# An encoder step on one core: the up projections by five matrix products a block in place of six, and the low-rank chunk by its high parts alone

## The chip, the cores and the metric

One core of a Trainium2 chip. The metric is the device time of one execution in microseconds, the median of three runs.

## The reference

Two layers over 544 tokens (512 of a prompt, 32 of a sample), width 1024, float32. Each layer normalises, mixes, adds, normalises again and goes through a gated feed-forward part. The odd layer's mixer has a forget gate of rank 16. Cut to what matters:

```python
def conv_ffn(h, conv_prev, w_up, conv_w, conv_b, w_down):
    gate, val = jnp.split(h @ w_up, 2, axis=-1)
    ext = jnp.concatenate([conv_prev.astype(h.dtype), gate], axis=1)
    conv = conv_b
    for j in range(CONV_W):
        conv = conv + ext[:, j:j + l] * conv_w[j]
    y = (jax.nn.gelu(conv) * val) @ w_down
    return y, ext[:, -(CONV_W - 1):]

# in odd_mixer: cr is h @ w_in's columns 1536 to 1551
log_a = jax.nn.log_sigmoid((cr @ w_gate2 + b_gate).astype(f32)) / GATE_NORM
```

w_up is 1024 x 5632 and w_down 2816 x 1024 in either layer.

## The kernel before

Activations lie with features on the 128 partitions and the 544 tokens along the free axis: a tensor of width 1024 is eight feature blocks of 128 x 544. Weights come as 187 slabs of 128 x 1024, each of which holds eight blocks of 128 x 128. SyncE loads a slab, GpSimd splits it into a high part `w_hi` and a low part `w_lo` (`split`, lines 392 to 395, into a ring of four slabs; it waits until TensorE has done the slab four places earlier), and TensorE multiplies it. All matrix products that use slabs are made of three products in the float32r type: high by high, high weight by low activation, low weight by high activation.

There are two ways to write the three products of one 128 x 128 block:

- `tiles` (lines 424 to 426): the 544 tokens are cut in two halves of 272, each half in a PSUM bank of its own, with three matmuls each, so six a block. All projections but the down projections use it.
- `tiles_apart` (lines 435 to 439): the tokens are cut in 304 (`ONE`) and 240 (`TWO`). The 304 take three matmuls. For the 240, one matmul of 480 columns multiplies the high weight by the high and the low activations side by side, into two separate areas of one bank, and one of 240 adds the low weight's part to the first area. So it is five a block, and whoever reads the result must add the two areas. The down projections use it (lines 1290 to 1294 add both areas to `x`).

An up projection of a layer is 22 gate slabs and 22 value slabs in turn. The four PSUM pairs are used in the order gate, value, gate, value of two chunks; TensorE may overwrite a pair once VectorE has read the chunk two before (`gate_out`, `val_out`). For each chunk VectorE (`ffn`, `chunk`, lines 1236 to 1271) scales the gate by `rstd` into a buffer with two columns of history before the prompt and before the sample, writes those edges, and forms the causal convolution of three taps (L1254, L1256, L1259). ScalarE takes the GELU (L893), VectorE scales the value (L1264), multiplies (L1267, L1268), ScalarE rounds to the high part (L898) and VectorE subtracts for the low part (L1271). Every order is written out by hand; each engine runs its own program and they meet in semaphores.

The odd mixer begins with slab 86, the low-rank chunk `cr`: 16 of its 128 output columns are not zero. Its block c waits until VectorE has written the low part of normalised block c (`norm_low`, L1190, announced by `h_ready`). Then the sum of squares is reduced (`total`, L448), the next slab follows, and behind it the product of the 16 rows of `cr` with the gate's second weight (L654). After slab n = 2 of this mixer VectorE runs, for both halves j of the gate, a prefix sum (L1508) with its subtractions (L1506, L1513), and only then evacuates slab n = 3 (L1480), which slab n = 5 waits for.

Of the kernel before, what the change touches and what calls it, by code (L numbers as in the profile page):

```python
# [22 lines left out]
F32 = mybir.dt.float32  # L23
# [64 lines left out]
def build(nc, io):  # L88
    ctx = ExitStack()
    with ctx:  # L90
# [128 lines left out]
        resets = sq[:, 0]  # L219
        o_s_in = sb("sample_state", [P, 256])  # L220
# [27 lines left out]
        w_hi_done, w_ready = sem("w_hi_done"), sem("w_ready")  # L248
# [26 lines left out]
        og_read, head_y = sem("og_read"), sem("head_y")  # L275
        conv_ready, y_f, y_ready = sem("conv_ready"), sem("y_f"), sem("y_ready")
# [104 lines left out]
        def _(pool):  # L381
# [33 lines left out]
        def _(pe):  # L415
# [59 lines left out]
            def ffn(layer, n_norm, upd0):  # L475
                s0, d0, f0 = S_UP[layer], S_DOWN[layer], FC * layer

                def up(i, k, fresh=False):
# [5 lines left out]
                    tiles(k, s0 + k, h_tiles(0, KC), True, True).then_inc(slab_done, 1)  # L484
# [362 lines left out]
        def _(ac):  # L847
# [37 lines left out]
            def ffn(layer, n_norm, upd0):  # L885
                s0, d0, f0, g0 = S_UP[layer], S_DOWN[layer], FC * layer, sums(n_norm + 1)

                def chunk(i, p):

                    f = 2 * i + p  # L890
                    ac.wait_ge(conv_ready, 2 * i + (f0 + p + 1))
# [121 lines left out]
            dma(o_wg[0:16, :], io["gate_w"], in_odd)  # L1013
# [156 lines left out]
        def _(ve):  # L1170
# [59 lines left out]
            def ffn(layer, n_norm, upd0):  # L1230
                s0, d0, f0 = S_UP[layer], S_DOWN[layer], FC * layer

                def chunk(i, p):
# [11 lines left out]
                    grouped(g, 2 * p, 2).then_inc(gate_out, 1)  # L1245
# [3 lines left out]
                    ve.tensor_copy(g[:, SEQ + 2:SEQ + 4].unsqueeze(1), conv_past[:, layer, one, :]).then_inc(vec, 1)  # L1249
# [555 lines left out]
```

## Time and profile before

| | us |
|---|---|
| median of 3 runs | 1280.73 |
| lowest and highest of them | 1280.19, 1281.85 |
| the profiled execution | 1279.63 |
| its span in the trace | 1277.5 |
| TensorE busy | 1223.4 (96% of the span) |
| VectorE busy | 807.4 (63%) |
| GpSimd busy | 699.6 (55%) |
| ScalarE busy | 261.8 (20%) |

A row of the timeline gives the start and the length of an instruction; matmuls overlap in it, so the pace of TensorE is the distance between starts, or a stretch divided by its count of matmuls. In a row of groups the mean of one instruction stands behind the busy time, and behind the bar stands the idle time of that engine before the group. L with a number is a line of the kernel before.

### The profile page before, as it was taken

How to read it: one execution, taken by the hardware profiler on the slowest of the kernel's cores; microseconds unless marked ns; L12 is line 12 of the kernel's file. 1: busy time of each engine (PE TensorE's matmuls, PEld its weight loads, DVE VectorE, ACT ScalarE, POOL GpSimd, SP SyncE). 2: the span in 40 equal slices, each digit the busy share in tenths (PEclk: the TensorE clock that was granted, in tenths of full speed). 3: DMA queues.
4: the chain of work that ended last, by engine and by line, in shares of the span. 5: the costliest groups of instructions: out<-in, count | busy, mean ns of one | idle time of the engine just before them, and what ended most of it. 6: DMA issues, size and time to landing. Idle time of an engine off the chain costs nothing.

```text
span 1277.5 us, 24157 instructions
## 1 busy us (share of the span) xinstructions
PE 1223.4 (96%) x9325; PEld 1178.8 (92%) x9325; DVE 807.4 (63%) x1206; ACT 261.8 (20%) x514; POOL 699.6 (55%) x565
## 2 busy tenths in 40 slices
PE   6978899999999999999999998899999999999995
PEld 6967799999999999999999986799999999999995
DVE  6987577778787731126534688766777777762222
ACT  3015332111111200002111165422111111110002
POOL 6732257655665666665653441256665566566661
PEclk9989999999999999999999999999999999999998
DMA  5311123222222223223222310132222222222221
GB/s 212 116 58 34 32 71 100 82 82 96 85 82 86 94 83 100 99 94 115 84 83 67 102 50 33 34 110 85 97 82 82 89 92 82 83 98 93 90 81 71
DMA packets 35522, 108.88 MB, mean 85 GB/s; under 512 B 5984, under 2 KB 7792, under 8 KB 35472
## 3 DMA queue, kind: packets, MB, share of 16 engines
q1 hardware_dynamic: 29232, 102.51, 24.0%
q10 hardware_dynamic: 6240, 5.64, 1.4%
q8 instruction: 39, 0.64, 0.2%
q14 instruction: 11, 0.09, 0.0%
HBM read 103.00 MB, written 5.13 MB: 85 GB/s over the span
## 4 chain that ended last, share of the span: by engine, by line
PE 87%; DVE 9%; ACT 2%; issue 1%; DMA 0%; POOL 0%; ACTq 0%; POOLq 0%; SPq 0%; DVEq 0%
PE psum L424 21%; PE psum L426 20%; PE psum L425 20%; PE psum L437 6%; PE psum L435 4%; PE psum L436 4%; PE psum L438 4%; PE psum L439 3%; DVE even_winsum L1358 1%; PE psum L754 1%; PE psum L621 1%; DVE small L1579 1%; DVE even_rope_swapped L1340 1%; ACT diff_probs L1091 0%; DVE even_diff L1361 0%
## 5 line engine op out<-in xcount | busy, mean ns | idle before, releaser
L424 PE MATMUL psum<-h_hi,w_hi 128*128 128x272 f32 x2032 | 593.7, 292 | 14.4 <-DVE h_lo L1190 10.3
L426 PE MATMUL psum<-h_hi,w_lo 128*128 128x272 f32 x2032 | 588.8, 290 | 0.0
L425 PE MATMUL psum<-h_lo,w_hi 128*128 128x272 f32 x2032 | 585.8, 288 | 0.0
L395 POOL TENSOR_TENSOR w_lo<-w_raw,w_hi 128x1024 fp32r<-128x1024 f32 x187 | 465.1, 2487 | 15.6
L424 PEld LDWEIGHTS psum<-h_hi,w_hi 128*128 128x128 f32 x2032 | 383.2, 189 | 19.6 <-issue 16.7
L425 PEld LDWEIGHTS psum<-h_lo,w_hi 128*128 128x128 f32 x2032 | 383.9, 189 | 0.2
L426 PEld LDWEIGHTS psum<-h_hi,w_lo 128*128 128x128 f32 x2032 | 383.1, 189 | 0.0
L392 POOL TENSOR_TENSOR tick<-tick 1x1 f32<-1x1 f32 x183 | 38.5, 210 | 523.7 <-PE psum L426 444.4
L393 POOL TENSOR_SCALAR w_hi<-w_raw 128x1024 fp32r<-128x1024 f32 x187 | 197.5, 1056 | 9.3 <-DMA w_raw<-in_weights 8.0
L437 PE MATMUL psum<-y_both,w_hi 128*128 128x480 f32 x352 | 133.4, 379 | 0.0
L1290 DVE TENSOR_TENSOR x<-x,psum 128x240 f32 (+1 forms) x16 | 6.4, 401 | 176.1 <-PE psum L439 176.0
L1254 DVE TENSOR_SCALAR conv<-gate,consts 128x546 f32<-128x546 f32 x44 | 104.1, 2366 | 7.0 <-DVE tails L1251 6.9
L435 PE MATMUL psum<-y_both,w_hi 128*128 128x304 f32 x352 | 107.7, 306 | 0.0
L436 PE MATMUL psum<-y_both,w_hi 128*128 128x304 f32 x352 | 106.4, 302 | 0.0
L438 PE MATMUL psum<-y_both,w_lo 128*128 128x304 f32 x352 | 105.4, 300 | 0.0
L439 PE MATMUL psum<-y_both,w_lo 128*128 128x240 f32 x352 | 95.7, 272 | 0.0
L1267 DVE TENSOR_TENSOR sq<-sq,conv 128x512 f32<-128x512 f32 x44 | 65.3, 1483 | 43.7 <-ACT conv L893 43.7
L439 PEld LDWEIGHTS psum<-y_both,w_lo 128*128 128x128 f32 x352 | 66.0, 188 | 10.2
L436 PEld LDWEIGHTS psum<-y_both,w_hi 128*128 128x128 f32 x352 | 66.9, 190 | 0.0
L437 PEld LDWEIGHTS psum<-y_both,w_hi 128*128 128x128 f32 x352 | 66.2, 188 | 0.0
L438 PEld LDWEIGHTS psum<-y_both,w_lo 128*128 128x128 f32 x352 | 66.1, 188 | 0.0
L435 PEld LDWEIGHTS psum<-y_both,w_hi 128*128 128x128 f32 x352 | 66.1, 188 | 0.0
(217 smaller groups left out, 1456.1 us busy)
## 6 DMA issues: line engine op xcount, KB each, us to landing
w_raw<-in_weights SPq DMA_DIRECT2D x187, 512.0 KB, 3.5
x<-in_x SPq DMA_DIRECT2D x8, 272.0 KB, 5.6
out_y<-x SPq DMA_DIRECT2D x8, 272.0 KB, 2.4
out_diff_v_new<-odd_dv ACTq DMA_DIRECT2D x1, 1024.0 KB, 6.2
out_diff_k_new<-odd_kT ACTq DMA_DIRECT2D x1, 1024.0 KB, 4.7
even_rope<-in_rope ACTq DMA_DIRECT2D x1, 544.0 KB, 3.9
odd_rope<-in_rope ACTq DMA_DIRECT2D x1, 544.0 KB, 3.6
consts<-in_consts ACTq DMA_DIRECT2D x1, 384.5 KB, 4.7
```

The costliest lines, as they stand in the source:

```text
L393: pool.tensor_scalar(w_hi[:, k], w_raw[:, k % RAW], 1.0, 0.0, ALU.mult, ALU.add).then_inc(w_hi_done, 1)
L395: pool.tensor_tensor(w_lo[:, k], w_raw[:, k % RAW], w_hi[:, k].bitcast(F32), ALU.subtract).then_inc(w_ready, 1)
L424: pe.matmul(out, wh, xh[:, cols], start=first and n == 0, stop=False)
L425: pe.matmul(out, wh, xl[:, cols], start=False, stop=False)
L426: ins = pe.matmul(out, wl, xh[:, cols], start=False, stop=last and n == len(pairs) - 1)
L435: pe.matmul(one, wh, both[:, 0, 0:ONE], start=first, stop=False)
L436: pe.matmul(one, wh, both[:, 1, 0:ONE], start=False, stop=False)
L437: pe.matmul(two, wh, both[:, :, ONE:T], start=first, stop=False)
L438: pe.matmul(one, wl, both[:, 0, 0:ONE], start=False, stop=last)
L439: return pe.matmul(two[:, 0], wl, both[:, 0, ONE:T], start=False, stop=last)
L1254: ve.tensor_scalar(c[:, :], g[:, 0:CO], tap(0), None, ALU.mult).then_inc(vec, 1)
L1267: ve.tensor_tensor(sq[:, p, 0:SEQ], sq[:, p, 0:SEQ], c[:, 0:SEQ], ALU.mult)
```

## The change

Four edits:

1. All slabs of the up projections go through `tiles_apart` (h's high and low parts become one tensor `h_both`). The value and the gate thus have a second area of 240 columns. ScalarE copies it from PSUM to SBUF (`gate_rest`, `val_rest`, in the space of `sumsq`), VectorE adds the copy to the first area in PSUM (`fold`) and scales from there.
2. The first tap moves from VectorE (L1254) to ScalarE, which waits for the edge columns (`edge_in`) and is waited for by the second tap (`tap_ready`).
3. The low-rank chunk: its weights are written twice, in columns 0 to 15 and 32 to 47. GpSimd overwrites the second copy's high part with the low part (one instruction, `stacked`), so four matmuls a block with 48 weight columns stand in for six. Rows 0 to 15 and 32 to 47 of the result are added in the gate's product, whose weight is stacked twice too.
4. The prefix sum of the gate's second half runs after slab n = 3 is evacuated, not before.

```diff
@@ gpsimd
-            with pool.Fori(1, NSLAB // RING) as i:
+            first_odd = S_ODD_IN // RING
+            with pool.Fori(1, first_odd + 1) as i:
+                for k in range(RING):
+                    split(i, k)
+            pool.wait_ge(w_ready, S_ODD_IN + 1)
+            cr = S_ODD_IN % RING
+            pool.tensor_scalar(w_hi[:, cr].rearrange("p (c m) -> p c m", c=KC)[:, :, 32:48],
+                               w_lo[:, cr].bitcast(F32).rearrange("p (c m) -> p c m", c=KC)[:, :, 0:16],
+                               1.0, 0.0, ALU.mult, ALU.add).then_inc(stacked, 1)
+            with pool.Fori(first_odd + 1, NSLAB // RING) as i:
@@ tensor
+            def low_rank(acc, s, c):
+                wh = w_hi[:, s % RING, c * P:c * P + 48]
+                for half in range(2):
+                    cols = slice(half * HALF, (half + 1) * HALF)
+                    out = psum[0:48, 2 * acc + half, 0:HALF]
+                    pe.matmul(out, wh, h_hi[:, c, cols], start=c == 0, stop=False)
+                    ins = pe.matmul(out, wh, h_lo[:, c, cols], start=False, stop=c == KC - 1)
+                return ins
...
+                    if n_norm and n == 0:
+                        pe.wait_ge(stacked, 1)
...
-                    tiles(k, s0 + k, h_tiles(0, KC), True, True).then_inc(slab_done, 1)
+                    for c in range(KC):
+                        ins = tiles_apart(k, s0 + k, c, h_both[:, :, c], c == 0, c == KC - 1)
+                    ins.then_inc(slab_done, 1)
...
-                        ins = tiles(k, s0 + k, h_tiles(c, c + 1), c == 0, c == KC - 1)
+                        ins = tiles_apart(k, s0 + k, c, h_both[:, :, c], c == 0, c == KC - 1)
@@ scalar, chunk of ffn
+                    ac.wait_ge(slab_done, 4 * i + (s0 + 2 * p + 1))
+                    ac.activation(gate_rest, psum[:, 4 * p + 1, TWO:2 * TWO], ACT.Copy).then_inc(gate_apart, 1)
+                    ac.wait_ge(edge_in, 2 * i + (f0 + p + 1))
+                    ac.activation(conv[p][:, :], gate[p][:, 0:CO], ACT.Copy,
+                                  scale=conv_w[:, layer, one, 0]).then_inc(tap_ready, 1)
...
+                    ac.wait_ge(slab_done, 4 * i + (s0 + 2 * p + 2))
+                    ac.activation(val_rest, psum[:, 4 * p + 3, TWO:2 * TWO], ACT.Copy).then_inc(val_apart, 1)
@@ vector, chunk of ffn
+                def fold(acc, rest):
+                    two = psum[:, 2 * acc + 1, 0:TWO]
+                    ve.tensor_tensor(two, two, rest, ALU.add).then_inc(vec, 1)
+                    return two
...
-                    grouped(g, 2 * p, 2).then_inc(gate_out, 1)
+                    ve.tensor_tensor(g[:, 2:2 + ONE], psum[:, 4 * p, 0:ONE], rstd[:, 0:ONE], ALU.mult)
+                    ve.wait_ge(gate_apart, 2 * i + (f0 + p + 1))
+                    two = fold(2 * p, gate_rest)
+                    ve.wait_ge(vec, at_ + 1)
+                    ve.tensor_tensor(g[:, 2 + ONE:2 + SEQ], two[:, 0:SEQ - ONE], rstd[:, ONE:SEQ], ALU.mult)
+                    ve.tensor_tensor(g[:, SEQ + 4:GE], two[:, SEQ - ONE:TWO], rstd[:, SEQ:T], ALU.mult).then_inc(gate_out, 1)
...
-                    ve.tensor_scalar(c[:, :], g[:, 0:CO], tap(0), None, ALU.mult).then_inc(vec, 1)
-                    ve.wait_ge(vec, at_ + 4)
+                    ve.wait_ge(tap_ready, 2 * i + (f0 + p + 1))
...
-                    ve.tensor_tensor(halves(sq[:, p]), pair(2 * p + 1), halves(rstd), ALU.mult).then_inc(val_out, 1)
+                    ve.tensor_tensor(sq[:, p, 0:ONE], psum[:, 4 * p + 2, 0:ONE], rstd[:, 0:ONE], ALU.mult)
+                    ve.wait_ge(val_apart, 2 * i + (f0 + p + 1))
+                    two = fold(2 * p + 1, val_rest)
+                    ve.wait_ge(vec, at_ + 5)
+                    ve.tensor_tensor(sq[:, p, ONE:T], two, rstd[:, ONE:T], ALU.mult).then_inc(val_out, 1)
@@ vector, odd mixer
-                if n == 2:
-                    for j in range(2):
+                if n in (2, 3):
+                    for j in (n - 2,):
```

The order of ScalarE in its loop over chunks, first of the two chunks of an iteration; `conv_61` and `conv_60` are the same convolution buffer. Before:

```order
L893 ISA [waits in_const,conv_ready]
L893 ACT_TABLE_LOAD
L893 ACTIVATE conv_61<-conv_61,consts 128x546
L898 ISA [waits in_const,y_f]
L898 ACTIVATE y_both<-sq 128x544
```

Now:

```order
L923 ACT_TABLE_LOAD
L923 ACTIVATE sumsq<-psum 128x240 [waits slab_done]
L924 ISA
L926 ISA [waits in_const,edge_in]
L926 ACTIVATE conv_60<-gate_58,consts 128x546
L930 ISA [waits in_const,conv_ready]
L930 ACT_TABLE_LOAD
L930 ACTIVATE conv_60<-conv_60,consts 128x546
L933 REGISTER_ALU
L934 ACTIVATE sumsq<-psum 128x240 [waits slab_done]
L937 ISA [waits in_const,y_f]
L937 ACTIVATE y_both<-sq 128x544
```

The copies and the first tap have come in, and a second table load stands ahead of the first copy; the copy of the value's area stands behind the GELU. The second chunk of an iteration has no table load, before and now.

The order of VectorE in the odd mixer about slabs n = 2 and n = 3; `gate_tmp_101` and `gate_tmp_102` before, `gate_tmp_100` and `gate_tmp_101` now, are the two halves of the gate. Before:

```order
L1478 SCALAR_TENSOR_TENSOR odd_gla_q<-psum,rstd 128x544 [waits slab_done]
L1506 SCALAR_TENSOR_TENSOR gate_tmp_101<-gate_tmp_101 128x544 [waits gate_l]
L1508 SCALAR_TENSOR_TENSOR gate_tmp_101<-sq,gate_tmp_101 128x544 [waits vec]
L1513 TENSOR_TENSOR gate_tmp_101<-gate_tmp_101 128x512 [waits vec]
L1513 TENSOR_TENSOR gate_tmp_101<-gate_tmp_101 128x32
L1506 SCALAR_TENSOR_TENSOR gate_tmp_102<-gate_tmp_102 128x544 [waits gate_l]
L1508 SCALAR_TENSOR_TENSOR gate_tmp_102<-sq,gate_tmp_102 128x544 [waits vec]
L1513 TENSOR_TENSOR gate_tmp_102<-gate_tmp_102 128x512 [waits vec]
L1513 TENSOR_TENSOR gate_tmp_102<-gate_tmp_102 128x32
L1480 TENSOR_TENSOR odd_gla_k<-psum,rstd 128x544 [waits slab_done] x2
```

Now:

```order
L1531 SCALAR_TENSOR_TENSOR odd_gla_q<-psum,rstd 128x544 [waits slab_done]
L1559 SCALAR_TENSOR_TENSOR gate_tmp_100<-gate_tmp_100 128x544 [waits gate_l]
L1561 SCALAR_TENSOR_TENSOR gate_tmp_100<-sq,gate_tmp_100 128x544 [waits vec]
L1566 TENSOR_TENSOR gate_tmp_100<-gate_tmp_100 128x512 [waits vec]
L1566 TENSOR_TENSOR gate_tmp_100<-gate_tmp_100 128x32
L1533 TENSOR_TENSOR odd_gla_k<-psum,rstd 128x544 [waits slab_done]
L1559 SCALAR_TENSOR_TENSOR gate_tmp_101<-gate_tmp_101 128x544 [waits gate_l]
L1561 SCALAR_TENSOR_TENSOR gate_tmp_101<-sq,gate_tmp_101 128x544 [waits vec]
L1566 TENSOR_TENSOR gate_tmp_101<-gate_tmp_101 128x512 [waits vec]
L1566 TENSOR_TENSOR gate_tmp_101<-gate_tmp_101 128x32
L1533 TENSOR_TENSOR odd_gla_k<-psum,rstd 128x544 [waits slab_done]
```

The evacuation of slab n = 3 now stands between the work on the two halves; that of n = 4 stands behind both, as before.

## Rows read from the trace of the kernel before

**Rows 1.** The page: its first line, and the chain that ended last, by engine.
```profile
span 1277.5 us, 24157 instructions
...
PE 87%; DVE 9%; ACT 2%; issue 1%; DMA 0%; POOL 0%; ACTq 0%; POOLq 0%; SPq 0%; DVEq 0%
```

**Rows 2.** TensorE in four stretches: up and down of either layer (length, busy, matmuls).
```profile
200.00:440.00 240.00, 240.00 (x1905) 1.00 0.27 87
450.00:570.00 120.00, 120.00 (x805) 1.00 0.29 97
885.00:1125.00 240.00, 240.00 (x1906) 1.00 0.26 87
1135.00:1255.00 120.00, 120.00 (x806) 1.00 0.26 83
```

**Rows 3.** Groups of VectorE while layer 0 projects up, 200 to 440 us.
```profile
L1254 DVE TENSOR_SCALAR conv<-gate,consts 128x546 f32<-128x546 f32 x20 | 47.2, 2358 | 3.2 <-DVE tails L1251 3.2
L1267 DVE TENSOR_TENSOR sq<-sq,conv 128x512 f32<-128x512 f32 x20 | 28.7, 1436 | 19.9 <-ACT conv L893 19.9
L1268 DVE TENSOR_TENSOR sq<-sq,conv 128x32 f32<-128x32 f32 x20 | 25.5, 1277 | 0.0
...
L1249 DVE COPY gate<-consts 128x2 f32 x19 | 10.0, 528 | 3.0 <-DVE gate L1200 3.0
```

**Rows 4.** Single lines of VectorE, all 44 times: shortest/median/longest ns.
```profile
L1254 DVE TENSOR_SCALAR conv<-gate,consts x44: 505/2452/2584, 195.2 to 1132.2; 128x546 f32<-128x546 f32 x44
...
L1267 DVE TENSOR_TENSOR sq<-sq,conv x44: 692/1056/2186, 202.5 to 1137.5; 128x512 f32<-128x512 f32 x44
...
L1268 DVE TENSOR_TENSOR sq<-sq,conv x44: 176/1279/2386, 203.1 to 1138.4; 128x32 f32<-128x32 f32 x44
```

**Rows 5.** Groups of ScalarE in the same stretch.
```profile
L893 ACT ACTIVATE conv<-conv,consts 128x546 f32<-128x546 f32 x20 | 15.1, 754 | 68.8 <-DVE conv L1259 68.7
L893 ACT ACT_TABLE_LOAD x11 | 14.1, 1283 | 79.6 <-DVE conv L1259 79.6
L898 ACT ACTIVATE y_both<-sq 128x544 f32 x20 | 13.2, 658 | 57.3 <-DVE sq L1268 57.3
```

**Rows 6.** Timeline about 308 us: GpSimd first, then VectorE (start us, us).
```profile
306.83 0.18 POOL L392 TENSOR_TENSOR tick<-tick 1x1 f32<-1x1 f32 x1 [2.39 <-PE psum L426]
...
308.11 2.70 POOL L395 TENSOR_TENSOR w_lo<-w_raw,w_hi 128x1024 fp32r<-128x1024 f32 x1
...
308.49 2.38 DVE L1268 TENSOR_TENSOR sq<-sq,conv 128x32 f32<-128x32 f32 x1
...
312.48 0.85 DVE L1200 TENSOR_TENSOR gate<-psum,rstd 128x272 f32<-128x272 f32 x3
```

**Rows 7.** Timeline of the first chunk of layer 1: VectorE, then TensorE.
```profile
578.14 0.46 DVE L1291 TENSOR_TENSOR x<-x,psum 128x304 f32 x1
578.52 0.39 DVE L1294 TENSOR_TENSOR x<-x,psum 128x240 f32 x1
580.19 1.83 DVE L1190 SCALAR_TENSOR_TENSOR h_lo<-x,consts,h_hi  x1 [1.28 <-ACT h_hi L863]
581.94 0.71 DVE L1181 TENSOR_TENSOR sumsq<-sumsq,sq 128x544 f32<-128x544 f32 x1
...
577.23 0.29 PE L424 MATMUL psum<-h_hi,w_hi 128*128 128x272 f32 x1
...
583.28 1.08 PE L448 MATMUL psum<-sumsq,consts 128*128 128x272 f32 x4
```

**Rows 8.** Timeline of the gate's scans: VectorE, then TensorE.
```profile
600.57 3.37 DVE L1508 TENSOR_TENSOR_SCAN gate_tmp<-sq,gate_tmp 128x544 f32<-128x544 f32 x1
...
610.36 1.34 DVE L1480 TENSOR_TENSOR odd_gla_k<-psum,rstd 128x544 f32<-128x544 f32 x2
...
610.50 0.29 PE L426 MATMUL psum<-h_hi,w_lo 128*128 128x272 f32 x1
611.22 0.36 PE L424 MATMUL psum<-h_hi,w_hi 128*128 128x272 f32 x1 [0.43 <-DVE odd_gla_k L1480]
```

More of the change, by code:

```diff
@@ L106, in build @@
         h_at = top[0]
-        h_hi = sb("h_hi", [P, KC, T], F32R)
-        h_lo_at = top[0]
-        h_lo = sb("h_lo", [P, KC, T], F32R)
+        h_both = sb("h_both", [P, 2, KC, T], F32R)
+        h_lo_at = h_at + KC * T * 4
+        h_hi, h_lo = h_both[:, 0], h_both[:, 1]
         y_at = top[0]
@@ L460, in in_projection @@
                             pe.wait_ge(h_ready, KC * n_norm + c + 1)
-                        ins = tiles(in_acc(n_norm == 0, n), s0 + n, h_tiles(c, c + 1), c == 0, c == KC - 1)
+                        if n_norm and n == 0:
+                            ins = low_rank(in_acc(False, n), s0 + n, c)
+                        else:
+                            ins = tiles(in_acc(n_norm == 0, n), s0 + n, h_tiles(c, c + 1), c == 0, c == KC - 1)
                         if n_norm == 0 and n == 2 and c == 1:
@@ L653, in odd_side @@
                         for half in range(2):
-                            ins = pe.matmul(psum[:, 2 * j + half, 0:HALF], o_wg[0:16, j * P:(j + 1) * P],
-                                            o_cr[0:16, half * HALF:(half + 1) * HALF], start=True, stop=True)
+                            ins = pe.matmul(psum[:, 2 * j + half, 0:HALF], o_wg[0:48, j * P:(j + 1) * P],
+                                            o_cr[0:48, half * HALF:(half + 1) * HALF], start=True, stop=True)
                     ins.then_inc(side_mm, 1)
@@ L890, in chunk @@
                     f = 2 * i + p
+                    one = slice(f, f + 1) if isinstance(i, int) else bass.ds(f, 1)
+                    ac.wait_ge(slab_done, 4 * i + (s0 + 2 * p + 1))
+                    ac.activation(gate_rest, psum[:, 4 * p + 1, TWO:2 * TWO], ACT.Copy).then_inc(gate_apart, 1)
+                    ac.wait_ge(edge_in, 2 * i + (f0 + p + 1))
+                    settle(ac)
+                    ac.activation(conv[p][:, :], gate[p][:, 0:CO], ACT.Copy,
+                                  scale=conv_w[:, layer, one, 0]).then_inc(tap_ready, 1)
                     ac.wait_ge(conv_ready, 2 * i + (f0 + p + 1))
@@ L1244, in chunk @@
                     settle(ve)
[L1245 removed]
+                    at_ = 10 * i + (vec0 + 5 * p)
+                    ve.tensor_tensor(g[:, 2:2 + ONE], psum[:, 4 * p, 0:ONE], rstd[:, 0:ONE], ALU.mult)
[4 more added lines that the diff above has]
+                    ve.tensor_tensor(g[:, SEQ + 4:GE], two[:, SEQ - ONE:TWO], rstd[:, SEQ:T], ALU.mult).then_inc(gate_out, 1)
                     ve.wait_ge(gate_out, 2 * i + (f0 + p + 1))
                     settle(ve)
[L1249 removed]
+                    ve.tensor_copy(g[:, SEQ + 2:SEQ + 4].unsqueeze(1), conv_past[:, layer, one, :]).then_inc(edge_in, 1)
                     ve.tensor_copy(tails[:, one, 0:2], g[:, SEQ:SEQ + 2].unsqueeze(1)).then_inc(vec, 1)
                     ve.tensor_copy(tails[:, one, 2:4], g[:, GE - 2:GE].unsqueeze(1)).then_inc(vec, 1)
[L1252 removed]
                     ve.wait_ge(vec, at_ + 3)
[L1254 to L1255 removed]
+                    ve.wait_ge(tap_ready, 2 * i + (f0 + p + 1))
                     ve.scalar_tensor_tensor(c[:, :], g[:, 1:1 + CO], tap(1), c[:, :], ALU.mult, ALU.add)\
                         .then_inc(vec, 1)
[L1258 removed]
+                    ve.wait_ge(vec, at_ + 4)
                     ve.scalar_tensor_tensor(c[:, :], g[:, 2:2 + CO], tap(2), c[:, :], ALU.mult, ALU.add)\
@@ L1767, in lay_out @@
     out["rope"] = rope.reshape(P, 2, T)
-    out["gate_w"] = f["gla_w_gate2"][0]
+    out["gate_w"] = np.zeros((48, 256), np.float32)
+    out["gate_w"][0:16] = out["gate_w"][32:48] = f["gla_w_gate2"][0]
     out["lambda"] = np.ascontiguousarray(np.broadcast_to(f["diff_lambda"][0].reshape(1, 256), (P, 256)))
```

15 lines of the change are left out of this document (8 added, 7 removed).

## The prediction

> **What bounds the kernel now.** I read the page's chain first: 87% of what ended last is TensorE, 9% VectorE [rows 1]. So an edit pays if it shortens TensorE's stream or one of its few waits, and costs if it makes TensorE wait. Next the stretches by engine: in both projections of the feed-forward part TensorE is busy all the time at a granted clock of 1.00, the 2.4 GHz level, so its pace is the length of a stretch over its matmuls [rows 2]. Then what runs beside it there: VectorE and ScalarE [rows 3 to 6]. Last the two places of the odd mixer that the other edits touch [rows 7, 8].
>
> **Edit 1, TensorE's side.** Going up takes 240 us for 1905 matmuls, 126.0 ns each; six make a block, so 755.9 ns. Going down takes 120 us for 805, 149.1 ns each; five make a block, 745.3 ns. Layer 1 reads the same (1906 and 806) [rows 2]. Both forms stream as many columns: 6 x 272 = 1632 and 3 x 304 + 480 + 240 = 1632. At 2.4 columns per ns that is 680 ns, so what is left is 12.7 ns per matmul in one form and 13.1 in the other: the change saves one such remainder a block, 10.6 ns. The up projections have 2 layers x 44 slabs x 8 blocks = 704 blocks: **7.5 us**, all on the path. It is the same instruction form on the same engine with operands of the same kind, so I take the down row as it is; the bounds are 10.6 and 12.7 ns a block, 7.5 to 8.9 us, if TensorE waits for nobody.
>
> The Trainium skill has a rule against this: "TensorE: Matmul & The Clock Gate", Back-to-back issue gap, gives a single matmul's gap as N/2.4 + 2.5 ns. By it a matmul saved is worth 2.5 ns, an estimate of 1.8 us in all instead of 7.5. The trace's down row disagrees, and the row decides.
>
> **Edits 1 and 2, VectorE's and ScalarE's side.** Does TensorE then wait? A chunk is two slabs, 16 blocks: 12.1 us before, 11.93 after. VectorE's gate read of the eleventh chunk starts at 312.48, while its slab ended just before GpSimd's small instruction at 306.83 [rows 6]: VectorE runs some 6 us behind, and reads without waiting for TensorE. TensorE waits for a buffer only two chunks on, so this has cost nothing.
>
> VectorE's chunk of 12.1 us holds waits that stand in the rows as long durations. L1254 takes 2.36 us on average and 0.51 at least, L1267 1.44 and 0.69, L1268 (32 columns) 1.28 and 0.18, L1249 (two columns) 0.53 against some 0.29 [rows 3, 4]. In the timeline L1268 starts at 308.49 and ends at 310.87, just as GpSimd's L395 ends at 310.81 [rows 6]. So such instructions sit out GpSimd's pass over the weights. They add 1.85 + 0.75 + 1.10 + 0.24 = 3.9 us, which leaves a bare chain of 8.2 us.
>
> What the change does to the bare chain, per chunk:
> - L1254 goes from VectorE: -0.5 bare, and 1.85 of sitting out with it.
> - The gate read was 0.85 in three pieces [rows 6]. It becomes 304 columns, 0.46, the fold of 240, 0.39, then 208 and 32 columns, at most 0.39 and 0.18 [rows 4, 7], with a handover of 0.1: +0.65.
> - The second tap waits for ScalarE's first tap, 0.75 [rows 5] with two handovers, less the two edge copies that run meanwhile: +0.65.
> - Value: VectorE now waits for GELU (0.75, in every second chunk behind a table load of 1.28) and behind it for the copy, about 0.4 (an estimate from 0.66 for 544 columns) [rows 5], and then folds and scales, 0.39 each [rows 7]. Start to product it was 0.72 plus an idle time of 19.9/20 = 1.0 [rows 3]; it becomes 2.9: +1.2.
> - A second table load per two chunks stands ahead of the gate's copy. It begins when ScalarE has rounded, VectorE is then busy for about 1.2 us with L1271 and 304 columns, and 1.28 + 0.4 are needed: +0.5 every second time, +0.25.
>
> The sum is 8.2 - 0.5 + 0.65 + 0.65 + 1.2 + 0.25 = 10.45 us bare, below 11.93 by 1.5. With the remaining waits on GpSimd at today's mean (2.1) it would be 12.5, above it. I take the first as the measure, for this reason: GpSimd's pass over slab s + 4 starts when TensorE has done slab s, so an instruction that sits it out ends at a time fixed by TensorE, however late VectorE was. A late VectorE waits less. I worked one pair of chunks through: the edge copy falls into L395 and ends with it, L1267 falls into the next L395, and each next gate read starts 0.3 to 2.2 us late against its place, without growing. So the lag stays near 6 to 8 us. Now val_out comes about 10.3 us after the gate read starts, and it is needed four slabs (23.9 us) after the gate's slab ends, so the lag may be 13.6. Cost: **0**, with VectorE's lateness hidden by the two spare buffers. The copies of the low parts and ScalarE's other work have room: it works 15.1 + 14.1 + 13.2 = 42 of these 240 us [rows 5].
>
> The down projection needs the last chunk only behind its first two accumulators' 16 blocks each, 24 us later; nothing there. GpSimd has one more small instruction and leaves its loop once; it rests 2.39 us a slab [rows 6] and is three slabs ahead: 0.
>
> **Edit 3.** 48 matmuls become 32: 16 x 126.0 ns = 2.0 us less of TensorE. But each block waits for its h_lo. The first block starts at 577.23 and the last h_lo is there at 580.19 + 1.83 = 582.02; before, block 8 began at 577.23 + 7 x 0.756 = 582.52 and did not wait. At 0.504 a block it would begin at 580.76, so it waits until 582.1 and ends at 582.6. Then L448 needs the sum of squares, ready at 581.94 + 0.71 = 582.65. It starts at 582.8 instead of 583.28 [rows 7]: **0.5 us**. The other 1.5 become a wait for VectorE. Bounds: 0.3 if a handover is slow, 2.0 if both chains before it move too.
>
> **Edit 4.** TensorE's gap before slab n = 5 is 611.22 - 610.50 = 0.72, less the usual 0.13: 0.6 us, ended by L1480 at 610.36, which stood behind both prefix sums [rows 8]. Now that evacuation stands between them. Next late would be the evacuation of n = 4, at 610 to 612.5, needed by TensorE only near 616. **0.6 us**; bounds 0 and 0.7.
>
> **Sum.** 7.5 + 0.5 + 0.6 = 8.6 us. The profiled execution took 1279.63 us around a span of 1277.5 and becomes 1271.0. It lay 1.1 below the median of 1280.73, so the median becomes **1272.1**.
>
> **Rivals.**
> A. VectorE's chain bounds the up stage, slower than before. Place: the second and third tap, which read two SBUF tensors, also fall into GpSimd's first pass (about 1.05 us), and the edge copy and L1267 keep sitting out at their mean. Then a chunk takes 12.5 + 1.0 = 13.5. A layer has 20 chunks after the first two; the lag may grow by 13.6 - 6 = 7.6 us before TensorE stalls: 20 x (13.5 - 11.93) - 7.6 = 24 us a layer, 48 in two, less 8.6: 1320. It decides from 12.3 us a chunk, and from 12.5 it eats the whole gain. For it: rows 3 show such waits on more than one line. Against it: the fixed end of each. 6%.
> The Trainium skill, "SBUF — State Buffer", Who interferes with whom, says that a VectorE instruction with two SBUF inputs contends with a GpSimd one that reads SBUF and blocks fully; the trace agrees for L1267 and L1268. By that rule the taps can be blocked too.
> B. The same with all waits at today's mean, 12.5 us a chunk: 20 x 0.57 - 7.6 = 3.8 us a layer, 7.6 in two, so 1279.7, no change that shows. 4%.
> C. The joined matmul of 480 gives less here than in the down projection, for example a fifth of the remainder of 12.7 ns: 1.8 + 1.1 = 2.9 us, 1277.8. For it nothing in the trace; against it rows 2. The same small figure follows if the edit did not do what it says; the row counts would show it. 4%.
> D. The low-rank chunk gives its full 2.0, and a saved block 12 ns in place of 10.6: 8.4 + 2.0 + 0.6 = 11.0, 1269.7. For it: the waits in rows 7 hang on a VectorE instruction of 1.83 that also sat out GpSimd. Against it: nothing ahead of it moves. 8%.
> The forecast itself has 78%: 1270.7 to 1273.5 with the bounds of edits 3 and 4 and of the runs' own spread.
>
> **How the numbers follow.** I predict 1272.1. The range takes in the forecast, most of D below, and above it small stalls up to half of B: 1269.8 to 1276.0. About 0.2% (2.6 us) is what a measurement of this kernel can tell from no change. The forecast, C and D are faster by more than that: 0.90. Within 0.2% is B: 0.04. Slower is A: 0.06.
>
> **What would show it.** In the trace of the changed kernel: the up stretch with five matmuls in 745 ns and no idle time (a block at 756 means C); the sum's matmul L448 about 5.5 us behind the first block of the low-rank chunk, where it was 6.05, with a wait of about 1.3 us before its last block; no gap before slab n = 5; on VectorE a chunk of 11.93 us, with the lag behind TensorE not growing past 13 us. The prediction is wrong if TensorE shows waits for gate_out or val_out (A, B), or if the first slabs of the up stage wait.

## The result and the profile after

| | before | changed |
|---|---|---|
| median, same comparison (us) | 1280.48 | 1288.28 |
| runs | 6 | 6 |
| profiled execution: span (us) | 1277.5 | 1286.6 |

The ratio is 1.006, 95% interval 1.005 to 1.007: slower by 7.8 us, which is small, under 1%, but clear of the noise. The forecast was 1272.1 us, with a range of 1269.8 to 1276.0.

The page of the changed kernel: its first line, the busy line of the engines, and the shares of the chain.

```profile
span 1286.6 us, 23189 instructions
...
PE 1219.6 (95%) x8605; PEld 1153.0 (90%) x8605; DVE 748.0 (58%) x1294; ACT 348.3 (27%) x668; POOL 718.4 (56%) x566
...
PE 87%; DVE 8%; ACT 2%; issue 2%; DMA 0%; POOL 0%; ACTq 0%; POOLq 0%; DVEq 0%; SPq 0%
```

TensorE's busy time fell by 3.8 us only, from 1223.4, and the span grew by 9.1, from 1277.5. So there is new idle time, and matmuls that ran slowly. TensorE by stretches, columns as in [rows 2] (length, busy, matmuls, granted clock):

```profile
200.00:440.00 240.00, 240.00 (x1610) 1.00 0.27 88
447.50:453.50 6.00, 6.00 (x23) 0.53 0.24 81
460.00:570.00 110.00, 110.00 (x738) 1.00 0.29 96
890.00:1130.00 240.00, 240.00 (x1610) 1.00 0.27 88
```

Up goes at 240/1610 = 149.1 ns a matmul, five a block, 745.3 ns, exactly the down row's pace [rows 2]; layer 1 reads the same. But in the six microseconds from 447.5 the granted clock is 0.53, little above its 1.2 GHz level, and only 23 matmuls fit; in the kernel before, the same six microseconds hold 42. TensorE's timeline where layer 0 turns from up to down:

```profile
441.82 0.27 PE L452 MATMUL psum<-h_both,w_lo 128*128 128x240 f32 x1
447.35 0.59 PE L448 MATMUL psum<-y_both,w_hi 128*128 128x304 f32 x1 [5.25 <-issue]
447.74 0.46 PE L449 MATMUL psum<-y_both,w_hi 128*128 128x304 f32 x1
```

The last matmul of up starts at 441.82, the first of down at 447.35. Five and a half microseconds of waiting, after which matmuls start 0.39 apart instead of 0.14. From the start of the last up block to that of the first of down it is 6.17 us, then from block to block 1.49, 1.38, 1.37, 1.37, 0.83 and 0.75 from there on: the first six take 12.6 us where 4.5 are due, so 8.1 are lost. Layer 1 has the same wait, 5.52 us from 1131.23. Two times 8.1 is 16.3 us. Whom did TensorE wait for? VectorE on chunk 20, the last but one:

```profile
436.63 0.47 DVE L1291 TENSOR_TENSOR gate<-psum,rstd 128x304 f32<-128x304 f32 x1
...
438.60 1.66 DVE L1300 COPY gate<-consts 128x2 f32 x1 [0.17 <-DVE gate L1296]
...
441.40 0.79 DVE L1305 SCALAR_TENSOR_TENSOR conv<-gate,consts,conv 128x546 f32<-128x546 f32 x1 [1.00 <-ACT conv L926]
442.33 1.61 DVE L1308 SCALAR_TENSOR_TENSOR conv<-gate,consts,conv 128x546 f32<-128x546 f32 x1
443.87 0.46 DVE L1313 TENSOR_TENSOR sq<-psum,rstd 128x304 f32<-128x304 f32 x1
446.39 0.42 DVE L1275 TENSOR_TENSOR psum<-psum,sumsq 128x240 f32<-128x240 f32 x1 [2.06 <-ACT sumsq L934]
446.84 0.41 DVE L1317 TENSOR_TENSOR sq<-psum,rstd 128x240 f32<-128x240 f32 x1
```

L1291 begins to read the gate, L1300 is the edge copy, L1305 and L1308 are the two taps, and L1317 scales the value's second part and announces `val_out` at 447.25. TensorE starts 0.1 us later. The same two ends, gate read and value read of chunk 20, in the kernel before:

```profile
433.54 0.84 DVE L1200 TENSOR_TENSOR gate<-psum,rstd 128x272 f32<-128x272 f32 x3
...
439.80 0.72 DVE L1264 TENSOR_TENSOR sq<-psum,rstd 128x544 f32<-128x544 f32 x1
```

There the value was read by 440.5, with TensorE going up until 445.8: a margin of 5.3 us. The line of the kernel that makes this a wait is in `down`, and is in both kernels: both accumulators of down, when j is 0 or 1, wait for `val_out` of chunk 20.

The totals are the matmuls that reduce the sum of squares (L448 before, L471 after; the last one of all is L838 before and L868 after). The distances between their starts divide the time better than the medians do, since the first 190 us alone ranged from 190.1 to 193.2 us over the profiled executions of these kernels. Worked out from the traces, one execution each:

| kernel | up and down of layer 0 | odd mixer | up and down of layer 1 |
|---|---|---|---|
| before | 392.62 | 291.97 | 386.57 |
| changed | 396.84 | 292.57 | 391.38 |
| e1_split | 388.69 | 292.60 | 383.21 |
| e2_late | 402.11 | 293.65 | 394.77 |
| e3_hoist | 394.49 | 292.46 | 390.20 |
| e4_hoist_split | 394.51 | 292.55 | 389.00 |
| f1_tap_back | 395.61 | 292.55 | 390.15 |
| f2_no_folds | 388.69 | 292.92 | 383.21 |
| f3_split_no_odd | 389.27 | 291.60 | 383.21 |
| f4_split_hoist | 388.70 | 292.87 | 383.21 |
| g1_edge_act | 388.68 | 292.84 | 383.21 |
| g2_no_e4 | 388.68 | 291.75 | 383.22 |
| g3_no_e3 | 389.27 | 292.25 | 383.22 |

The first column also holds the odd mixer's low-rank chunk.

### The profile page after: what moved, and what is told of

The parts are those of the page before. It is cut to its first block, busy times and chain, and to the rows that moved or that the text cites. A ratio compares the mean times of both kernels' runs of the same rounds, so it can differ in the third digit from the quotient of the medians.

```text
span 1286.6 us, 23189 instructions
## 1 busy us (share of the span) xinstructions
PE 1219.6 (95%) x8605; PEld 1153.0 (90%) x8605; DVE 748.0 (58%) x1294; ACT 348.3 (27%) x668; POOL 718.4 (56%) x566
## 4 chain that ended last, share of the span: by engine, by line
PE 87%; DVE 8%; ACT 2%; issue 2%; DMA 0%; POOL 0%; ACTq 0%; POOLq 0%; DVEq 0%; SPq 0%
PE psum L450 18%; PE psum L448 12%; PE psum L449 12%; PE psum L451 11%; PE psum L452 9%; PE psum L437 7%; PE psum L439 6%; PE psum L438 6%; DVE even_winsum L1411 1%; PE psum L784 1%; PE psum L651 1%; DVE small L1632 1%; DVE even_rope_swapped L1393 1%; ACT diff_probs L1130 0%; DVE even_diff L1414 0%
## 5 line engine op out<-in xcount | busy, mean ns | idle before, releaser
L398 POOL TENSOR_TENSOR w_lo<-w_raw,w_hi 128x1024 fp32r<-128x1024 f32 x187 | 476.5, 2548 | 15.6
L450 PE MATMUL psum<-h_both,w_hi 128*128 128x480 f32 x704 | 267.0, 379 | 0.0
L448 PE MATMUL psum<-h_both,w_hi 128*128 128x304 f32 x704 | 215.8, 307 | 0.0
L449 PE MATMUL psum<-h_both,w_hi 128*128 128x304 f32 x704 | 212.9, 302 | 0.0
L451 PE MATMUL psum<-h_both,w_lo 128*128 128x304 f32 x704 | 210.9, 300 | 0.0
L437 PE MATMUL psum<-h_both,w_hi 128*128 128x272 f32 x608 | 180.5, 297 | 14.5 <-DVE h_both L1229 10.8
L452 PE MATMUL psum<-h_both,w_lo 128*128 128x240 f32 x704 | 191.5, 272 | 0.0
L439 PE MATMUL psum<-h_both,w_lo 128*128 128x272 f32 x608 | 176.4, 290 | 0.0
L438 PE MATMUL psum<-h_both,w_hi 128*128 128x272 f32 x608 | 175.5, 289 | 0.0
L452 PEld LDWEIGHTS psum<-h_both,w_lo 128*128 128x128 f32 x704 | 131.8, 187 | 20.3
L449 PEld LDWEIGHTS psum<-h_both,w_hi 128*128 128x128 f32 x704 | 133.7, 190 | 0.1
L437 PEld LDWEIGHTS psum<-h_both,w_hi 128*128 128x128 f32 x608 | 115.0, 189 | 19.4 <-issue 16.2
L448 PEld LDWEIGHTS psum<-h_both,w_hi 128*128 128x128 f32 x704 | 132.3, 188 | 0.1
L450 PEld LDWEIGHTS psum<-h_both,w_hi 128*128 128x128 f32 x704 | 132.3, 188 | 0.0
L451 PEld LDWEIGHTS psum<-h_both,w_lo 128*128 128x128 f32 x704 | 132.2, 188 | 0.0
L448 PE MATMUL psum<-y_both,w_hi 128*128 128x304 f32 x352 | 109.4, 311 | 10.5 <-issue 10.5
L438 PEld LDWEIGHTS psum<-h_both,w_hi 128*128 128x128 f32 x608 | 115.3, 190 | 0.1
L439 PEld LDWEIGHTS psum<-h_both,w_lo 128*128 128x128 f32 x608 | 115.0, 189 | 0.0
```

The source lines that it names most:

```text
L398: pool.tensor_tensor(w_lo[:, k], w_raw[:, k % RAW], w_hi[:, k].bitcast(F32), ALU.subtract).then_inc(w_ready, 1)
L437: pe.matmul(out, wh, xh[:, cols], start=first and n == 0, stop=False)
L438: pe.matmul(out, wh, xl[:, cols], start=False, stop=False)
L439: ins = pe.matmul(out, wl, xh[:, cols], start=False, stop=last and n == len(pairs) - 1)
L448: pe.matmul(one, wh, both[:, 0, 0:ONE], start=first, stop=False)
L449: pe.matmul(one, wh, both[:, 1, 0:ONE], start=False, stop=False)
```

## The experiments

The lag, below, is the time from the end of a chunk's gate slab to the start of VectorE's read of it. Theory 1: the whole loss is the wait for the value read of chunk 20, and the slow clock behind it. Rivals: VectorE is too slow for the stage and TensorE will wait for it elsewhere; or ScalarE's tap, not the folds, is what made VectorE late.

**e1_split.** The changed kernel, with the two accumulators' waits told apart. The first overwrites the banks of chunk 20's gate, the second those of its value, 16 blocks later.

```diff
-                                pe.wait_ge(val_out, f0 + FC - 1)
+                                pe.wait_ge(val_out if j else gate_out, f0 + FC - 1)
```

> The changed kernel; the first accumulator of the down projection waits for the gate read of chunk 20 (gate_out), the second for its value read (val_out); before, both waited for the value read. Theory 1 (the whole loss is this wait: VectorE reads that value 5.5 us after the last up matmul, and TensorE then runs five blocks at the lower clock; from 441.8 us on six block distances take 12.6 us where 4.5 are due, 8.1 us a layer): 1288.3 - 16.3 = 1272.0. Rival (VectorE is simply too slow for the stage, and TensorE will wait for it elsewhere, on y_ready or on buffers): 1280 or more.

Measured: 1272.79 us against 1280.36, ratio 0.9939 (0.9923 to 0.9956). TensorE at the same turn, and under it VectorE's gate and value reads of chunk 20:

```profile
442.38 0.27 PE L452 MATMUL psum<-h_both,w_lo 128*128 128x240 f32 x1
442.49 0.30 PE L448 MATMUL psum<-y_both,w_hi 128*128 128x304 f32 x1
442.63 0.30 PE L449 MATMUL psum<-y_both,w_hi 128*128 128x304 f32 x1
```

```profile
437.18 0.47 DVE L1291 TENSOR_TENSOR gate<-psum,rstd 128x304 f32<-128x304 f32 x1
...
447.40 0.41 DVE L1317 TENSOR_TENSOR sq<-psum,rstd 128x240 f32<-128x240 f32 x1
```

Down follows up at the usual 0.11 us. VectorE is as late as in the changed kernel, its value read ends at 447.81, 5.3 us after down began, and nobody waits for it: the second accumulator begins at 442.49 + 16 x 0.746 = 454.4. The up-and-down stretches are shorter than the changed kernel's by 8.15 and 8.17 us, as worked out above. Theory 1 holds, and this version is faster than both kernels.

**e2_late.** The kernel before, with a wait at this place and nothing else of the change.

```diff
-                                pe.wait_ge(val_out, f0 + FC - 1)
+                                pe.wait_ge(val_out, f0 + FC)
```

> The kernel before, whose down projection waits for the value read of chunk 21 in place of chunk 20. Prices an idle time of TensorE at this place without any of the change's edits. VectorE reads that value at 452.5, TensorE arrives at 445.7: 6.9 us of waiting. Theory 1 (a wait here costs its length and then some 2.6 us at the lower clock): 2 x 9.5 = 19 us, 1299.5. Rival (the slow blocks in the changed kernel have another cause, for example late y_ready): 2 x 6.9 = 14 us, 1294.3.

Measured: 1300.39 us against 1280.36, ratio 1.0159 (1.0142 to 1.0176).

```profile
446.74 0.29 PE L426 MATMUL psum<-h_hi,w_lo 128*128 128x272 f32 x1
453.63 0.59 PE L435 MATMUL psum<-y_both,w_hi 128*128 128x304 f32 x1 [6.60 <-issue]
```

A wait of 6.9 us cost 402.11 - 392.62 = 9.5 us in layer 0, so 2.6 went to slow blocks, as expected. In layer 1, with the same 6.9, it was 8.2. In the six microseconds from the first matmul of down the granted clock was 0.52 in layer 0 and 0.76 in layer 1. So the slow blocks belong to the wait, not to the new kernel. Over all the traces with a wait here, what came on top of it varied from 1.3 to 2.7 us.

**e3_hoist.** The changed kernel with ScalarE's GELU table loaded ahead of the loop. Copy is in that table too, so none is left inside.

```diff
                 rms(n_norm, 3)
+                load_tables(11)
                 with ac.Fori(0, FC // 2) as i:
```

> The changed kernel with one table load ahead of ScalarE's loop over chunks and none inside (both functions are in that table). In even chunks the value read then ends 1.3 us earlier and the gate read 0.4. Theory 1a (VectorE's place is held by GpSimd's passes, 12 to 13 us behind its slab): the stall falls from 5.5 to some 4 us a layer, 1285 to 1286. Theory 1b (the two loads in the first chunk are what made VectorE fall a whole pass further behind): the lag is 6 us again, no stall, 1272.

Measured: 1284.75 us against 1280.36, ratio 1.0038 (1.0024 to 1.0052).

```profile
441.83 0.27 PE L452 MATMUL psum<-h_both,w_lo 128*128 128x240 f32 x1
446.09 0.52 PE L448 MATMUL psum<-y_both,w_hi 128*128 128x304 f32 x1 [3.99 <-issue]
```

The wait falls by 1.27 us, one table load, and no more. VectorE's lag (reckoned from the start of up at 5.965 us a slab) is 12.9 to 13.3 us; in the changed kernel it went to and fro between 12.9 and 14.4. So the loads explain the last microsecond of it, and not the pass by which VectorE is late.

**e4_hoist_split** is, against its name, the same kernel as e3_hoist a second time.

> The same kernel as e3_hoist once more, for one look at how alike two traces of one kernel are in VectorE's lag. Both theories: the same lag as in e3_hoist within 0.5 us, time within 0.3%.

Measured, in one run: 1285.3 us, the wait 4.30 against 4.26, the lags equal within 0.2 us. So the lag is no accident of one execution. What the wait costs is less steady: layer 1 took 389.00 us here and 390.20 in e3_hoist, with the same wait of 4.26.

**f1_tap_back.** The changed kernel with edit 2 undone.

```diff
-                    ac.wait_ge(edge_in, 2 * i + (f0 + p + 1))
-                    settle(ac)
-                    ac.activation(conv[p][:, :], gate[p][:, 0:CO], ACT.Copy,
-                                  scale=conv_w[:, layer, one, 0]).then_inc(tap_ready, 1)
...
+                    ve.tensor_scalar(c[:, :], g[:, 0:CO], tap(0), None, ALU.mult).then_inc(tap_ready, 1)
```

> The changed kernel with the first tap back on VectorE, and ScalarE without it (edit 2 undone). Theory 1 (VectorE's added wait for GELU, copy and fold at the value, 3.6 us, and a first chunk that ends one GpSimd pass later, put the value read behind the end of the up stage): the tap's place matters little, since the 2.8 us from edge copy to second tap become an edge copy and a tap that sit out GpSimd; stall 4 to 7 us a layer, 1285 to 1291. Rival (the handover to ScalarE for the tap is what costs the pass): the lag is 6 us, no stall, 1272.

Measured: 1287.0 us against 1280.55, ratio 1.0049 (1.0033 to 1.0064).

```profile
442.65 0.27 PE L452 MATMUL psum<-h_both,w_lo 128*128 128x240 f32 x1
448.18 0.59 PE L448 MATMUL psum<-y_both,w_hi 128*128 128x304 f32 x1 [5.26 <-issue]
```

In layer 0 it is 5.53 us again, and the lag 13 to 14. In layer 1 the lag settles at 12.9 to 13.3 and the wait is 4.46 us (1130.81 to 1135.27). So with the first tap on VectorE a stall of 4.5 to 5.5 us stays: the handover to ScalarE is not what makes it.

**f2_no_folds.** ScalarE's two copies and VectorE's two folds are left out, so a part of the low products of 240 tokens is missing from the result.

```diff
-                    ve.wait_ge(gate_apart, 2 * i + (f0 + p + 1))
-                    two = fold(2 * p, gate_rest)
-                    ve.wait_ge(vec, at_ + 1)
+                    two = psum[:, 4 * p + 1, 0:TWO]
```

> The changed kernel without ScalarE's copies and VectorE's folds; the second area of 240 columns is not added, so its low parts are left out of the result. The tap stays on ScalarE. Theory 1: the value read ends some 3 us earlier after its gate read and ScalarE has one table load per two chunks again; no stall at the start of down, 1271 to 1273. Rival (the tap's handover): the stall stays at 3 us or more a layer, 1281 or more.

Measured: 1274.56 us against 1280.55, ratio 0.9947 (0.9932 to 0.9962), 1.6 us above the expected 1273 at most, a miss of the time; the profiled execution's first total starts at 193.15, where e1_split's starts at 190.69, and its up-and-down stretches equal e1_split's. No wait at down. VectorE's first two gate reads:

```profile
195.76 0.48 DVE L1287 TENSOR_TENSOR gate<-psum,rstd 128x304 f32<-128x304 f32 x1 [6.94 <-ACT rstd L904]
...
206.71 0.47 DVE L1287 TENSOR_TENSOR gate<-psum,rstd 128x304 f32<-128x304 f32 x1
```

Here the first chunk takes 10.95 us, in the changed kernel 16.3. From the third chunk on the lag is 6.0 to 6.7, a whole slab less, with the tap still on ScalarE. So the copies and folds, with what they bring along, are enough to make VectorE late, and the tap alone is not. They are not the only thing that can be taken away: g1_edge_act below keeps them and has the short lag.

**f4_split_hoist.** e1_split with e3_hoist's edit.

> The kernel e1_split with one table load ahead of ScalarE's loop and none inside. Theory 1: once TensorE waits for nobody at the start of down, VectorE's lag costs nothing, so the loads are free: 1272.8, the same as e1_split within 0.5 us. Rival (the lag still costs TensorE somewhere): 1 us or more faster.

Measured: 1273.77 us, ratio 0.9948 (0.9935 to 0.9962), 1.0 us above e1_split where 0.5 at most was expected. The interval overlaps e1_split's, and the profiled execution's first total starts 1.0 us later (191.71 against 190.69). The up-and-down stretches equal e1_split's within 0.01 us. The loads are free once nobody waits, and so is the lag.

**g1_edge_act.** e3_hoist, with the edge copy on ScalarE.

```diff
+                    settle(ac)
+                    ac.activation(gate[p][:, SEQ + 2:SEQ + 4].unsqueeze(1), conv_past[:, layer, one, :],
+                                  ACT.Copy).then_inc(edge_in, 1)
                     ac.wait_ge(edge_in, 2 * i + (f0 + p + 1))
+                    ac.wait_ge(gate_out, 2 * i + (f0 + p + 1))
...
-                    ve.tensor_copy(g[:, SEQ + 2:SEQ + 4].unsqueeze(1), conv_past[:, layer, one, :]).then_inc(edge_in, 1)
```

> The kernel e3_hoist (down still waits for the value read) with the copy of the two edge columns of the gate moved from VectorE to ScalarE, ahead of its first tap; the tap then waits for gate_out. Theory P (VectorE's place two slabs behind is held by the edge copy, which sits out GpSimd's pass for 1.5 us each time): VectorE catches up, its lag falls to 7 us or less, no stall, 1272 to 1273. Rival (another instruction that reads two SBUF tensors, the second or third tap, takes the place of the copy at the same pass): the lag stays at 11 to 13 us and the stall at 2.5 to 4.3 us a layer, 1281 to 1285.

Measured: 1273.86 us against 1281.76, ratio 0.9948 (0.9933 to 0.9962). VectorE at the first chunk, then at chunk 20:

```profile
194.09 0.48 DVE L1296 TENSOR_TENSOR gate<-psum,rstd 128x304 f32<-128x304 f32 x1 [6.94 <-ACT rstd L904]
...
196.67 1.62 DVE L1305 COPY tails<-gate 128x2 f32<-128x2 f32 x1
...
199.22 1.60 DVE L1312 SCALAR_TENSOR_TENSOR conv<-gate,consts,conv 128x546 f32<-128x546 f32 x1
...
205.19 0.47 DVE L1296 TENSOR_TENSOR gate<-psum,rstd 128x304 f32<-128x304 f32 x1
```

```profile
431.54 0.47 DVE L1296 TENSOR_TENSOR gate<-psum,rstd 128x304 f32<-128x304 f32 x1
...
438.94 0.41 DVE L1321 TENSOR_TENSOR sq<-psum,rstd 128x240 f32<-128x240 f32 x1
```

No stall, lag 6.4 to 6.7. Theory P forecast the time, but its mechanism is only half right. The next copy (L1305, two columns of `tails`) takes the edge copy's place and sits GpSimd out just as long, 1.62 us and later 2.3. What changed is that the second tap no longer waits for a ScalarE tap that waits for that copy: it starts 4.3 us behind the first gate read, where it was 5.2 in e3_hoist. The first chunk then ends after 11.1 us instead of 16.0, a pass of GpSimd earlier, and VectorE stays one pass further ahead from there on.

Where that pass is won or lost can be seen on the third tap of the first chunk (L1308 in the changed kernel, L1312 here) and on GpSimd's L398, the pass that reads the weights for the low part. In the changed kernel and here:

```profile
198.55 2.75 POOL L398 TENSOR_TENSOR w_lo<-w_raw,w_hi 128x1024 fp32r<-128x1024 f32 x1
```

```profile
200.32 2.75 POOL L398 TENSOR_TENSOR w_lo<-w_raw,w_hi 128x1024 fp32r<-128x1024 f32 x1
```

In the changed kernel the third tap starts at 199.08, 0.53 us behind the start of L398, and takes 2.81 us. Here it starts at 199.22, 1.1 us ahead of L398, and takes 1.60. All 26 first chunks in the traces (13 kernels, two layers) fall the same way. In the 18 where the tap comes 0.5 us behind the start of L398 it takes 2.81 and the lag is the long one; in the 8 where it comes 1.0 to 1.1 us ahead (the kernel before, e2_late, f2_no_folds and this one) it takes 1.45 to 1.60 and the lag is the short one. f1_tap_back, which has no tap on ScalarE, is among the 18: its second tap took 1.59 us, where g1_edge_act's took 0.79. So the lag is set in the first chunk and then kept. That the third tap's start decides it is read from the traces; no run moved that tap alone.

**f3_split_no_odd, g2_no_e4, g3_no_e3.** These are e1_split with both edits 3 and 4 undone (f3), with only edit 4 undone (g2) and with only edit 3 undone (g3). Below, the first cut undoes edit 4; the second is the main line of what undoes edit 3.

```diff
-                if n in (2, 3):
-                    for j in (n - 2,):
+                if n == 2:
+                    for j in range(2):
...
-                        if n_norm and n == 0:
-                            ins = low_rank(in_acc(False, n), s0 + n, c)
-                        else:
-                            ins = tiles(in_acc(n_norm == 0, n), s0 + n, h_tiles(c, c + 1), c == 0, c == KC - 1)
+                        ins = tiles(in_acc(n_norm == 0, n), s0 + n, h_tiles(c, c + 1), c == 0, c == KC - 1)
```

> The kernel e1_split with edits 3 and 4 undone (low-rank chunk by six matmuls of 128 weight columns a block; both prefix sums behind slab n = 2). The prediction's terms: edit 3 is worth 0.5 us, edit 4 0.6, so 1.1 us above e1_split: 1273.9. In the trace the distance from the odd mixer's first matmul to its second slab is 6.76 again, and the gap before slab n = 5 0.72. Rival (edit 3 gives the full 2.0): 2.6 us above, 1275.4.

> The kernel e1_split with edit 4 alone undone. From total to total, the odd mixer with its attention takes 291.97 us in the kernel before, 292.57 in the changed kernel, 292.60 in e1_split and 291.60 in f3_split_no_odd, though TensorE is 0.6 us ahead at slab n = 5 in the second and third. Theory (edit 4 gives 0.66 there, and the attention, which meets GpSimd's passes 0.6 us earlier, gives back 1.4): this stretch takes 291.6 to 292.0 again and the time is 1271.6 to 1272.5. Rival (edit 3's shift does it): 293.2, and 1273.4.

> The kernel e1_split with edit 3 alone undone. Theory of g2: the stretch from total to total still takes 292.6, and the first chunk of the odd mixer costs 0.6 us more: 1273.4. Rival: the stretch takes 291.0, 1271.7.

Measured: 1273.55 (ratio 0.9944, 0.9931 to 0.9958), 1274.14 (0.9949, 0.9936 to 0.9962) and 1274.08 (0.9944, 0.9931 to 0.9956). The intervals of all three and of e1_split overlap, so by the medians neither edit is worth anything that shows; g2_no_e4 missed its expected 1271.6 to 1272.5, and g3_no_e3 came 0.7 above its 1273.4. The stretches say more. Edit 3 is worth 389.27 - 388.69 = 0.58 us, in two pairs alike. With edit 4 TensorE runs 0.6 us ahead after slab n = 5, and yet the odd mixer takes 292.60 with it (e1_split) and 291.75 without (g2_no_e4). e1_split keeps its lead until 236 us behind the start of this stretch, in the attention, and then loses 1.5 us. Below are a window of e1_split and one of g2_no_e4 at the same work: length; busy time and count of TensorE's matmuls, its weight loads, VectorE, ScalarE and GpSimd; then the granted clock and the DMA:

```profile
816.10:819.50 3.40, 3.40 (x15) 2.66 (x16) 1.51 (x5) 1.13 (x8) 0.00 (x0) 0.50 0.34 140
816.30:819.70 3.40, 3.40 (x22) 2.43 (x22) 2.19 (x8) 1.87 (x10) 0.00 (x0) 1.00 0.54 154
```

The granted clock was 0.50, the 1.2 GHz level, in e1_split and 1.00 in g2_no_e4: 15 matmuls against 22, and GpSimd does nothing in either window. So what was expected, an attention that meets GpSimd's passes at a worse moment, is not what the trace shows there. Such stretches at 0.50 stand in the odd mixer of every trace but f3_split_no_odd's, which has the shortest mixer (291.60); e2_late, with 293.65, and f2_no_folds, with 292.92, have the most. Whether edit 4 brings them on stays open: e2_late's odd mixer is the kernel before's own code, and it took 293.65 where the kernel before took 291.97. The mixer's length moves by that much with what came before it.

## Why the prediction was wrong

**TensorE's gain from edit 1** was right in kind and pace: 745.3 ns a block, the down row's. In the stretches it is 386.57 - 383.21 = 3.36 us in layer 1 where 3.73 were reckoned, so 6.7 us in both instead of 7.5. Rival C is refuted by the 745.3 ns. So is the estimate of 1.8 us from the Trainium skill, "TensorE: Matmul & The Clock Gate", Back-to-back issue gap; the section gives the formula behind it for an isolated matmul, and a matmul saved in this stream was worth about 10 ns.

**The step that failed** is "The down projection needs the last chunk only behind its first two accumulators' 16 blocks each, 24 us later; nothing there." It looked at `y_ready` alone. The line beside it makes the first block of down wait for the value read of chunk 20. Inside up, a pair is needed again four slabs after the gate's slab ends, 23.9 us; at the end of up, the first down block comes after three, 17.9 us. The bound on VectorE's lag was therefore not 13.6 us but 17.9 - 10.3 = 7.6. The runs show what it cost: a wait of 5.5 us at the first block of down in either layer, and 8.15 us a layer in all, which e1_split takes away by that one line. The prediction's own sign of being wrong, a wait for `val_out`, did come, but at down and not inside up.

**The second miss is the size of the lag.** The prediction put it near 6 to 8 us. It was 12.9 to 14.4. The value read came 10.6 us after the gate read of chunk 20 (436.63 to 447.25), as reckoned (10.3), and the groups of VectorE over the same stretch as [rows 3] are near the sum too:

```profile
L1308 DVE SCALAR_TENSOR_TENSOR conv<-gate,consts,conv 128x546 f32<-128x546 f32 x20 | 32.6, 1628 | 2.7 <-DVE conv L1305 0.2
L1300 DVE COPY gate<-consts 128x2 f32 x19 | 26.5, 1394 | 3.1 <-DVE gate L1296 3.1
L1275 DVE TENSOR_TENSOR psum<-psum,sumsq 128x240 f32<-128x240 f32 x40 | 16.5, 412 | 32.9 <-ACT sumsq L934 28.6 <-ACT sumsq L923 4.3
...
L1320 DVE TENSOR_TENSOR sq<-sq,conv 128x512 f32<-128x512 f32 x20 | 15.9, 797 | 0.7
```

L1308, the last tap, and L1300, the edge copy, now sit out GpSimd (1.63 and 1.39 us on average where 0.79 and 0.17 are their shortest), and little else does: some 2.2 us a chunk beside the 2.1 of today's mean, which the prediction had set aside for rival B. VectorE's chunk took 23.9/2 us, so the argument that instructions which sit out GpSimd tie VectorE to TensorE's slabs was right for the pace: the lag did not grow. It was wrong on the lag at which it starts. The first chunk in the changed kernel:

```profile
192.75 0.47 DVE L1291 TENSOR_TENSOR gate<-psum,rstd 128x304 f32<-128x304 f32 x1 [6.94 <-ACT rstd L904]
...
195.33 1.65 DVE L1300 COPY gate<-consts 128x2 f32<-128x2 f32 x1
...
199.08 2.81 DVE L1308 SCALAR_TENSOR_TENSOR conv<-gate,consts,conv 128x546 f32<-128x546 f32 x1
...
204.34 0.42 DVE L1275 TENSOR_TENSOR psum<-psum,sumsq 128x240 f32<-128x240 f32 x1 [2.07 <-ACT sumsq L934]
...
205.23 2.24 DVE L1320 TENSOR_TENSOR sq<-sq,conv 128x512 f32<-128x512 f32 x1
...
209.03 0.47 DVE L1291 TENSOR_TENSOR gate<-psum,rstd 128x304 f32<-128x304 f32 x1
```

From gate read to gate read it takes 16.3 us, before 12.4 (193.27 to 205.63 in that trace). The fold waits for a table load (1.15 us), the edge copy sits out a pass (1.65), the last tap too (2.81), the value waits 2.07 for ScalarE, and L1320 meets yet another pass (2.24). The prediction worked one pair of chunks in the middle through, not the first one, which begins behind with rstd. With the true bound of 7.6, a lag of 6 to 8 would have cost half a microsecond at most; with the true lag of 13.1, a bound of 13.6 would have cost nothing. It took both: 13.1 + 10.6 - 17.9 = 5.8 us, measured 5.5 (the reckoned slab ends lie about half a microsecond early).

**The price of a wait** had no term: behind 5.5 us of idle time come blocks at 1.38 us, 2.7 us more a layer.

**Rival A** named the right engine and the right sign, but another place and mechanism: a chunk slower than TensorE's in steady state. That never happened. Its 1320 was far off.

**Edit 3** was right: TensorE waits before its last block for the last h_lo (L460 at 586.33), and the sum's matmul comes 5.5 us behind the first block (581.47 to 586.97):

```profile
581.47 0.29 PE L460 MATMUL psum<-h_both,w_hi 128*48 128x272 f32 x1
...
584.83 0.29 PE L461 MATMUL psum<-h_both,w_hi 128*48 128x272 f32 x1
586.33 0.33 PE L460 MATMUL psum<-h_both,w_hi 128*48 128x272 f32 x1 [1.21 <-DVE h_both L1229]
...
586.97 1.18 PE L471 MATMUL psum<-sumsq,consts 128*128 128x272 f32 x4
```

Reckoned 0.5 us, measured 0.58; rival D's full 2.0 is out. **Edit 4** was right at its place, no gap is left before slab n = 5, and wrong as a term of the sum: of its 0.6 us nothing shows at the end of the odd mixer, where stretches at the lower clock had come in; why is open.

The sum 1272.1 comes close to what the change does once the wait is split: e1_split took 1272.8. That is in part luck: edit 1 gave 0.8 us less than its term, and the gain of edit 4 did not last.

## What to carry to other kernels

An engine that runs behind without being waited for has a bound, and the bound must be read at every wait on it, above all where a stage ends and buffers are reused in another order. Work the first pieces of a stage through, not only the steady state: a lag from the start may stay to the end. A wait written for the later of two buffers is cheap to tell apart, and here was worth 15.5 us (1288.28 to 1272.79).

## What the runs showed of the hardware

TensorE waited 5.5 us at the turn from up to down. In the six microseconds from 447.5 the granted clock was then 0.53, and 23 matmuls ran where the kernel before ran 42. Behind waits of 4.3 to 6.9 us at this place such slow blocks came in every trace, but the extra cost was 1.3 to 2.7 us and not the same for the same wait: behind 6.9 us of waiting the granted clock over six microseconds was 0.52 in one layer of e2_late and 0.76 in the other.

VectorE's two-column edge copy took 0.17 us at its shortest in the changed kernel, and 1.66 in the median of its 44 times and 2.19 at most, beside GpSimd's pass; in g1_edge_act the first copy of `tails`, as small, took 2.28 in the median. The third tap, 0.79 us at its shortest, took 2.81 when it started 0.5 us behind the start of the pass. With such waits VectorE's lag stood at one slab or at two from the fifth chunk on: 6.0 to 6.7 or 12.9 to 14.4 us, nothing between, in all the traces.
